# Two banks for transposed probabilities in the layers, and block 1's banded heads woven into their projections

## The reference, cut to what matters

```python
sq = partial_rope(rms_norm(grp(swa_q), q_norm_w), cos, sin)      # 3 groups x 4 heads
sk = partial_rope(rms_norm(grp(swa_k), k_norm_w), cos, sin)
...
merged = jax.nn.sigmoid(g_dn) * y_dn + jax.nn.sigmoid(g_swa) * y_swa
x = x + merged @ w_out
```

## Time and profile before

| | us |
|---|---|
| median of 3 runs | 3165.8 |
| lowest and highest | 3159.13 and 3172.29 |
| the profiled execution | 3162.07 |
| span inside the profiled execution | 3160.3 |

### The profile page before, as it was taken

The page is one execution under the profiler, slowest core; times in us unless marked ns, Lnnn a source line. Parts: engine busy times, 40 slices in busy tenths (PEclk is TensorE's granted clock), DMA queues, the critical chain, the costliest instruction groups (busy, mean ns, idle before and its releaser), DMA issues.

```text
span 3160.3 us, 36642 instructions
## 1 busy us (share of the span) xinstructions
PE 2952.1 (93%) x13424; PEld 2334.4 (74%) x13424; DVE 1468.4 (46%) x2032; ACT 1088.7 (34%) x1771; POOL 237.6 (8%) x176
## 2 busy tenths in 40 slices
PE   8878898999899999998999999899999988999998
PEld 5567676678678888566768888788886666778886
DVE  5653246853354433555444443444434545354432
ACT  4412233444223222555343332323224645332321
POOL 0000000000110012000220002100021000120012
PEclk9989899999999999999999999999999999999999
DMA  3100221213322333011212232232322110222332
GB/s 118 53 14 14 70 74 34 73 40 96 111 80 93 102 101 136 17 48 34 66 55 93 93 104 100 69 100 93 105 92 100 40 41 27 74 77 96 98 102 79
DMA packets 68356, 237.97 MB, mean 75 GB/s; under 512 B 10272, under 2 KB 12448, under 8 KB 67616
## 3 DMA queue, kind: packets, MB, share of 16 engines
q1 hardware_dynamic: 66240, 227.87, 22.3%
q10 hardware_dynamic: 2016, 8.77, 0.7%
HBM read 234.51 MB, written 2.10 MB: 75 GB/s over the span
## 4 chain that ended last, share of the span: by engine, by line
PE 65%; ACT 3%; DVE 3%; issue 2%; DMA 0%; POOLq 0%; DVEq 0%; POOL 0%; SPq 0%; PEldq 0%; ACTq 0%
PE bank L372 18%; PE bank L374 18%; PE bank L373 18%; PE bank L823 2%; PE bank L847 2%; PE bank L834 2%; PE bank L630 2%; PE bank L640 1%; PE bank L1427 1%; ACT L_w_hi L360 1%; ACT L_probsT L900 1%; PE bank L1404 0%; ACT L_job_rstd L673 0%; DVE L_h_lo L467 0%; ACT L_probs L889 0%
## 5 line engine op out<-in xcount | busy, mean ns | idle before, releaser
L372 PE MATMUL bank<-L_h_hi,L_w_hi 128*128 128x512 f32 x1776 | 703.2, 396 | 36.8 <-DVE L_weight_ring_low L366 14.0
L374 PE MATMUL bank<-L_h_hi,L_weight_ring_low 128*128 128x512 f32 x1776 | 694.8, 391 | 0.0
L373 PE MATMUL bank<-L_h_lo,L_w_hi 128*128 128x512 f32 x1776 | 694.5, 391 | 0.0
L360 ACT CAST L_w_hi<-L_weight_ring 128x1024 fp32r<-128x1024 f32 (+2 forms) x292 | 325.9, 1116 | 924.4 <-PE bank L374 915.6
L366 DVE TENSOR_TENSOR L_weight_ring_low<-L_weight_ring,L_w_hi 128x1024 fp32r<-128x1024 f32 (+2 forms) x292 | 393.8, 1349 | 380.1 <-ACT L_w_hi L360 379.7
L372 PEld LDWEIGHTS bank<-L_h_hi,L_w_hi 128*128 128x128 f32 x1776 | 335.4, 189 | 116.0 <-DVE L_weight_ring_low L366 15.7
L373 PEld LDWEIGHTS bank<-L_h_lo,L_w_hi 128*128 128x128 f32 x1776 | 335.9, 189 | 70.6 <-issue 2.4
L374 PEld LDWEIGHTS bank<-L_h_hi,L_weight_ring_low 128*128 128x128 f32 x1776 | 335.3, 189 | 70.8
L372 PE MATMUL bank<-L_act_hi,L_w_hi 128*128 128x512 f32 x704 | 273.9, 389 | 0.0
L373 PE MATMUL bank<-L_act_lo,L_w_hi 128*128 128x512 f32 x704 | 273.9, 389 | 0.0
L374 PE MATMUL bank<-L_act_hi,L_weight_ring_low 128*128 128x512 f32 x704 | 273.9, 389 | 0.0
(11 more groups left out here) (304 smaller groups left out, 3891.9 us busy)
## 6 DMA issues: line engine op xcount, KB each, us to landing
L_weight_ring<-ffn_in SPq DMA_DIRECT2D x176, 512.0 KB, 3.6
L_weight_ring<-ffn_out SPq DMA_DIRECT2D x64, 704.0 KB, 4.1
B_weight_ring<-w_sqk SPq DMA_DIRECT2D x24, 512.0 KB, 3.6
B_weight_ring<-w_dn SPq DMA_DIRECT2D x16, 512.0 KB, 3.7
B_weight_ring<-w_gate SPq DMA_DIRECT2D x16, 512.0 KB, 3.6
L_weight_ring<-w_sna_qk SPq DMA_DIRECT2D x16, 512.0 KB, 3.7
L_weight_ring<-w_mix_out SPq DMA_DIRECT2D x16, 512.0 KB, 3.6
B_weight_ring<-w_sv SPq DMA_DIRECT2D x12, 512.0 KB, 3.6
```

The source lines that it names most:

```text
L360: e.copy(hv.high(at)[:, 0:width], sh.ring[:, at % RING, 0:width]).then_inc(hv.w_hi_done, 1)
L372: e.matmul(out, a_hi, b_hi, start=start, stop=False)
L373: e.matmul(out, a_hi, b_lo, start=False, stop=False)
L374: return e.matmul(out, a_lo, b_hi, start=False, stop=stop)
```

## The change

**In the layers.** Turned probabilities go through banks 3 and 1 in turn (`at_.pt_done` starts with a credit of 2). Jobs from the sixth on all use bank 0 (`job["bank"] = 0`), and so a projection waits until DVE has read the one before it. From step 6 to 24 (`sums_first`, the new argument `early`) each engine finishes job j-1 before it begins job j. The first unit's transposes wait until the last job that used bank 1 has been read (`turn_needs`).

**In block 1.** The loop over two pairs of heads is gone. Four heads of six jobs and four units stand in one list, `sw_turns`: seven jobs and a unit; three times job, job, unit, job, job, unit, job, unit, job, unit; four units. A head's first scores wait for that head's six jobs. At steps 12, 18 and 24 the finish stands in front (`sw_first`). Jobs use banks 0 and 1 and one sum bank, 2; turned probabilities use bank 3 alone, outputs bank 4. Within a unit step the segments of `scores(u+1)` alternate with the groups of transposes of `turn(u)` (`zip_longest`); ACT and DVE run one unit ahead, not two.

**Output projection of block 1.** It writes banks 0 and 1 instead of 4 and 5. Its first tile starts when seven merged tiles are there and waits for the eighth before its last three matmuls.

```diff
-def jobs_pe_steps(e, seen, sh, jb, at, jobs, hv=None, mixed=False):
+def jobs_pe_steps(e, seen, sh, jb, at, jobs, hv=None, mixed=False, early=(), sum_banks=None):
...
+        for turn in (("finish", "begin") if j in early else ("begin", "finish")):
+            if turn == "begin" and j < len(jobs):
...
+                bank = banks[job.get("bank", j % 2)]
+                e.wait_ge(jb.gained, seen.free(jb.gained) + ("bank" in job))
...
     for u in range(n):
+        turned, scored = turn(u), scores(u + ahead) if u + ahead < n else ()
         if ahead == 2:
-            turn(u)
-        if u + ahead < n:
-            scores(u + ahead)
-        if ahead == 1:
-            turn(u)
+            for _ in itertools.chain(turned, scored):
+                pass
+        else:
+            for _ in itertools.zip_longest(scored, turned):
+                pass
...
-        at_ = Attn(sc, T, [4, 5], [3], [6, 7], big, 8 * TT)
+        at_ = Attn(sc, T, [4, 5], [3, 1], [6, 7], big, 8 * TT)
...
+            for job in mix_jobs[5:]:
+                job["bank"] = 0
...
+            mix_units[0]["turn_needs"] = [(jb.gained, jobs_before + 4)]
+            mem_units[0]["turn_needs"] = [(jb.gained, jobs_before + len(mix_jobs) + 4)]
...
+        sums_first = range(6, 2 * MLA_HEADS + 8 + 1)
...
-        at_ = Attn(sc, 1280, [5, 6, 7], [0, 1], [2, 3], big)
+        at_ = Attn(sc, 1280, [5, 6, 7], [3], [4], big)
...
+                                     needs=[(jb.done, 2 + 8 + 4 + 6 * (h + 1))] if t == 0 else []))
...
+        sw_turns = ["job"] * 7 + ["unit"]
+        sw_turns += ["job", "job", "unit", "job", "job", "unit", "job", "unit", "job", "unit"] * (NH - 1) + ["unit"] * TT
+        sw_first = range(2 * len(sw_jobs) // NH, len(sw_jobs) + 1, len(sw_jobs) // NH)
...
-                e.wait_ge(merged_done, seen.ready(merged_done, KT))
+                all_merged = seen.ready(merged_done, KT)
                 for n in range(KT):
                     e.wait_ge(sh.x_done, seen.free(sh.x_done))
                     halves_here(e, seen, sh, hv, at + n)
                     for k in range(KT):
-                        mm = halves_mm(e, banks[4 + n % 2][:, :], hv, at + n, k, merged_hi[:, k, :],
+                        if n == 0 and k in (0, KT - 1):
+                            e.wait_ge(merged_done, all_merged - (k == 0))
+                        mm = halves_mm(e, banks[n % 2][:, :], hv, at + n, k, merged_hi[:, k, :],
```

More of the change, by code:

```diff
@@ L18 @@
+import itertools
 from contextlib import ExitStack, contextmanager
@@ new lines, in jobs_act_steps @@
+        for turn in (("finish", "begin") if j in early else ("begin", "finish")):
+            if turn == "begin" and j < len(jobs):
+                job = jobs[j]
+                r0, rn = job["rows"]
+                w = job["width"]
+                e.wait_ge(sh.strip_done, seen.ready(sh.strip_done, len(job["parts"])))
+                e.wait_ge(jb.summed, seen.free(jb.summed))
+                src = sh.banks[job.get("bank", j % 2)][r0:r0 + rn, 0:w]
+                if "by" in job:
+                    e.wait_ge(jb.gained, job["number"])
+                    src = jb.g[r0:r0 + rn, j % 2, 0:w]
+                e.activation(jb.sq[r0:r0 + rn, j % 2, 0:w], src, ACT.Square).then_inc(jb.squared, 1)
+                if hv is not None and job.get("split", True):
+                    split_strip_act(e, seen, sh, hv, at + j + 2, KT * P)
+            if turn == "finish" and j > 0:
+                job, b = jobs[j - 1], (j - 1) % 2
+                w = job["width"]
+                e.wait_ge(jb.summed, seen.ready(jb.summed))
+                e.wait_ge(jb.done, seen.free(jb.done))
+                e.activation(jb.rs[:, b, 0:w], sh.banks[sum_banks[b % len(sum_banks)]][:, 0:w], ACT.Ln, scale=job["scale"],
+                             bias=EPS).then_inc(jb.lned, 1)
+                e.wait_ge(jb.lned, seen.ready(jb.lned))
+                e.activation(jb.rs[:, b, 0:w], jb.rs[:, b, 0:w], ACT.Exp, scale=-0.5).then_inc(jb.rstd, 1)
@@ L824, in scores @@
             seg[0] += 1
-        if units[u]["segs"][0][3] is not None:
-            seen.free(at_.exped)
+            yield
     def turn(u):
         e.wait_ge(at_.exped, seen.ready(at_.exped))
+        for need in units[u].get("turn_needs", ()):
+            e.wait_ge(*need)
         for ch in chunks(units[u]):
@@ L904, in attn_act_steps @@
     n = len(units)
-    for u in range(2):
+    ahead = 2 if len(units[0]["segs"]) == 1 else 1
+    for u in range(ahead):
         exps(u)
@@ L983, in attn_dve_steps @@
     yield
-    for u in range(2, n + 2):
+    for u in range(ahead, n + ahead):
         if u < n:
@@ L2425, in _ @@
                         e.copy(val[:, t, bass.ds(it * 512, 512)], banks[4 + t][:, :]).then_inc(v_done, 1)
-                j_, a_ = jl(0), al()
-                with seen.loop(e, 2, ready=merged(j_[2], a_[2]), free=merged(j_[3], a_[3])) as it:
-                    jobs_act(e, seen, sh, jb, sw_jobs, hv, V_FIRST + 12)
-                    attn_act(e, seen, sh, at_, units(it))
+                take_turns(sw_turns, job=jobs_act_steps(e, seen, sh, jb, sw_jobs, hv, V_FIRST + 12, sw_first, (2,)),
+                           unit=attn_act_steps(e, seen, sh, at_, sw_units))
                 for f in range(NH):
```

275 lines of the change are left out of this document (122 added, 153 removed).

## The result

| | us |
|---|---|
| before, median of 4 runs | 3165.4 (3159.13 to 3172.29) |
| after, median of 4 runs | 3129.5 (3127.07 to 3138.72) |
| ratio, 95% interval | 0.9903, 0.9891 to 0.9916 |
| the profiled execution after, its span | 3127.07, 3125.2 |
| after once more (experiment 5), median of 5, and before beside it, median of 9 | 3135.8, before 3161.7 |

The change makes the kernel about 0.9% faster; the second pair says 26 us, the first ratio 31. One of the ten executions of experiment 6 took 9455 us, for a reason that no run shows, and is left out there; all others agree with their like within 0.5%. The page of after: PE does the same 13424 matmuls, and the span is 35.1 us shorter.

What follows compares the result with a forecast made beforehand. PE was taken to bound the kernel, busy 93% of the span, with gains only where it waits. From 3162.1, 25 for the layers and 6.7 for the output projection came off, 0 for the weave: 3130 us, range 3106 to 3153.

Steps and rivals of the forecast that it cites:

- two of three terms: The sum's terms: 25 us off in the two layers, 6.7 off at the output projection, 0 for the weave.
- Part 1, long jobs: Layers, after long jobs: three copy waits go, five windowed ones keep 3.4 of 8.9 us; gain 9.3 us per layer.
- The early finish: Layers: Ln and Exp move ahead of ACT's square, taking 1.16 us off ACT's path to the copy.
- 3.5 against 3.1: Layers, full unit: PE wants the copy 3.5 us after a job's end; ACT's copy ends at 3.1.
- first rival: Layers: the copy is missed again, at the values; only 1.16 us go at eight places, 18.6 in all, 3137; chance 0.17.
- Part 2, units after the jobs: Layers, units behind the jobs: the second bank saves 3.2 of 7.0 us of waits per layer, bounds 0 and 7.0.
- Part 3, short jobs: Layers, short jobs: almost no PE wait there, so moving the sum gains zero, bounds -2 and +2 us.
- Part 4, output projection: Block 1: the gap shrinks to 0.6 us, saving 4.8, and absent half-clock matmuls return 1.9; gain 6.7, bounds 4.8 and 7.3.
- Part 5, the weave: Block 1: idle time 29.1 us against 28.0 before, so the weave is worth nothing, within -13 and +12.
- I expect two falls again: Block 1's weave: the clock falls twice as before, now at gaps of 5.8 and 6.8 us.
- The rule: Layers: the skill's remark that PSUM double-buffering gave no further gain with PE busy; by it the time would be 3137.

Runs made afterwards that it cites:

- experiment 5: The changed kernel with block 1's attention as before (no weave): 3129.9 us, run beside the unaltered changed kernel at 3135.8.
- experiment 6: Only block 1's output projection changed, against the kernel before: 3154.6 us against 3160.3, ratio 0.9985.
- experiment 2: Kernel before with the layers' edits but begin before finish everywhere, so the second bank without the early finish: 3133.4 us, ratio 0.9920 to before.
- experiment 3: Kernel before with the layers' edits but transposed probabilities through bank 3 alone, so the early finish without the second bank: 3160.0 us, ratio 0.9994.
- after_again: The changed kernel, unaltered, run and profiled once more: 3135.8 us against 3161.7 for before, ratio 0.9915.
- experiment 1: Kernel before with all of the layers' edits, block 1 untouched: 3136.7 us against 3161.7, ratio 0.9927.
- experiment 10: The changed kernel with two banks for block 1's turned probabilities and two instead of three for its scores: 3175.8 us, ratio 1.0056 to before.
- experiment 7: The changed kernel with the finish in front also at head 0 (step 6 of block 1): 3126.2 us against 3160.3 of before, ratio 0.9891.
- experiment 9: The changed kernel with the finish in front at head 0 too and head 3's last jobs each a unit earlier: 3132.5 us, ratio 0.9908 to before.

## Why the prediction was right, and where it wasn't

The forecast was 3130 us; the measured median is 3129.5, and 3135.8 in the second set of runs. The direction and two of three terms hold; the third was hidden by the spread. That the first median meets the forecast to 0.5 us is luck: its distance from before is 35.9 us in this set and 25.9 in the second, and the forecast takes off 32.

**Part 1, long jobs: 9.3 us per layer.** Right in mechanism. The three waits of 1.25 went; at the five windowed places 0.22, 0.33, 0.66, 2.42 and 0.66 remain, 4.3 for 3.4. The 2.42 was not foreseen: the forecast counted ACT's steps and left out that DVE's new order can make ACT's square late (experiment 2). The period is 10.66 (10.9 forecast). That a projection waits for bank 0 did not occur.

**The early finish** stands in the forecast as one of the two edits that make the gain, with 1.16 us off ACT's path. This is a step that failed inside a right sum. PE's sum moves away together with Ln and Exp, so PE comes 0.86 us earlier as well. The forecast has both shifts in its 3.5 against 3.1, but does not draw from them that only 0.3 us is left of the edit; without it the two would be 4.3 against 4.28. Three of the places of experiment 2 show that 0.3, and by the ratios the edit brings nothing that can be measured (experiments 2 and 3). With it falls the first rival's price of 18.6 us, which counted the 1.16 alone.

**Part 2, units after the jobs: 3.2 of 7.0.** 5.1 us remain in the first layer behind the last job's, so 1.9 were saved. The reason was right (the exponential comes right after the copy, 14.2 for 6.7), its size not. Parts 1 and 2 are thus 8.4 + 1.9 = 10.3 us of idle per layer, for 12.5 forecast. The second execution of the changed kernel shows just this (10.4 and 10.9). In the first another 1.6 per layer came from the wait for the residual, which fell from 5.5 to 2.4. That gain is not steady: over the ten executions with the second bank this wait is 2.4 to 5.5 us, and 5.5 in four besides `after_again`. What no term of the sum had is the cross-attention. It takes 58.3 us in either layer of before and 56.4 or 56.5 in after; over all executions it is 57.3 to 58.5 with one bank and 56.3 to 57.5 with two, so it gave 1 to 2 us per layer. That 25 us were forecast for the two layers and 25 measured (experiment 1) is in part luck.

**Part 3, short jobs: nothing.** Right; no wait stands between 1294 and 1411 us of after.

**Part 4, output projection: 6.7.** The gap fell to 0.6 and its half-clock matmuls are gone; the stage gives 6.7 in the trace and the time 5.7 (2 to 8) in the runs. The size is right, its make-up less so. Most of what the clock returned here it took later: from 855.3 us on PE is busy 1.6 us more up to the layers, and over the whole stage its busy time is only 0.3 less (590.32 to 590.02). In its place the waits for `L_h_lo` fell from 13.3 to 11.6, which was in no term. In experiment 6 it is the other way round: 1.4 us less of busy time, and 12.7 of these waits.

**Part 5, the weave: 0 (-13 to +12).** Measured +6, inside the bounds. The waits came as listed: 5.61, 0.66, 0.65 and 6.13 at the keys (5.8, 1.4, 1.4, 6.8 forecast), some 6.6 for the single bank in woven units (4.8), 6.2 in the tail (7.6), 1.0 at the store (1.3): 26.9 for 29.1. The step that failed is "I expect two falls again". In after the clock falls a third and a fourth time in the tail, at 654 and at 662, behind gaps of 2.08 and 2.15 us among small matmuls. The third:

```profile
653.61 0.66 PE L845 MATMUL bank<-shared_consts,B_arena 128*128 128x128 f32 x4 [2.08 <-ACT B_arena L903]
654.11 1.10 PE L833 MATMUL bank<-B_arena 128*128 128x512 f32 x2
...
655.91 1.92 PE L833 MATMUL bank<-B_arena 128*128 128x512 f32 x2
```

An equal pair of scores takes 1.10 and then 1.92 us. From 662 to 668 the granted clock is 0.50 again. `after_again` shows four falls as well, before and the kernel without the weave two. Over the stretch PE was busy for 3.9 to 5.6 us more than before, which the sum had at nothing.

**The rule.** The waits of transposes for copies, 39.8 us, fell with a second bank, and experiment 2 puts 25 us (by the ratio) to 28 (by the medians) on that edit. The Trainium skill's remark in "TensorE: Matmul & The Clock Gate", section "HAM oscillation — how this bites in real kernels", that PSUM double-buffering gave no further gain, is told of another matmul kernel; it is not what this one shows. The Trainium skill's "Perfetto Trace Analysis", section "Matmuls", says that independent groups should rotate through banks so that the emptying of one lies beside the next; experiment 2 agrees with it for the transposes, and experiment 10 for the scores, which lost a bank.

**The parts and the whole.** Layers -25.0, output projection -5.7 and weave +6.0 make -24.7 in medians; the changed kernel has -25.9 in the second pair and -35.9 in the first, where before ran at 3165.4 for the 3160 to 3162 of the others. So the parts add, and the first pair flattered the whole. The forecast's 32 us lies above both 26 and the 31 of the ratio. Why the changed kernel itself ran at 3129.5 once and at 3135.8 once no run shows; in the two profiled executions PE's busy time makes 4.8 of the 8.7 us between the spans.

**A better version.** Without the weave the kernel is 6 us below the changed one (3129.9 for 3135.8 on one chip, 0.9898 of before). With the weave and experiment 7's order it stands at 0.9891. The two were not run on one chip, so which is better stays open. Only the kernel without the weave is shown to be below the changed one; experiment 7's interval (0.9874 to 0.9907) overlaps with the changed kernel's.

## What to carry to other kernels

Before counting what leaves the releasing engine's path, count what leaves the waiting engine's path with it: a step that moves both wins only the difference. A second bank pays where the engine that empties the first has a long piece of other work to do first (here 2.6 to 3.7 us on ACT). A bank taken away from scores cost all that stood before the mask on DVE (up to 4.8 us), not the mask. And a rebuilt order is to be judged by idle time and by busy time: here waits fell and the stretch grew longer.

## What the runs showed of the hardware

One gap can be cheaper than its parts. In experiment 9 the longest wait of block 1 was cut up, idle time fell by 1.2 us, and 998 matmuls took 217.75 us where 997 had taken 211.25, at a mean granted clock of 0.94 for 0.97 (one execution each). In the tail of after the clock stood at its upper level while PE was only half busy, and fell right behind:

```profile
650.00:654.00 4.00, 1.92 (x14) 1.39 (x12) 2.11 (x3) 1.44 (x3) 0.00 (x0) 1.00 0.01 2
654.00:656.00 2.00, 2.00 (x10) 1.30 (x9) 0.69 (x1) 0.59 (x1) 0.00 (x0) 0.73 0.00 0
656.00:658.00 2.00, 2.00 (x5) 0.97 (x5) 0.14 (x1) 0.59 (x1) 0.00 (x0) 0.50 0.00 0
```

So the fall shows in matmuls that themselves wait for nothing.

The same work takes a different time from one execution to the next, and where no edit is at work the difference is busy time of PE. The first 430 us, up to the first sum of block 1, are alike in all kernels of this case. Their shortest and longest execution, those of experiment 10 and of before:

```profile
0.00:427.40 427.40, 361.22 (x1792) 280.56 (x1793) 192.92 (x280) 125.42 (x186) 0.20 (x4) 0.94 0.16 56
0.00:435.20 435.20, 370.57 (x1792) 285.89 (x1793) 192.94 (x280) 125.64 (x186) 0.21 (x4) 0.92 0.17 55
```

PE is busy for 9.4 us more at a granted clock of 0.92 for 0.94, and idle for 1.5 us less. The second mix took 272.5 to 275.5 us in the ten executions with the second bank. A stretch that differs by a few us between two profiled executions is therefore to be compared over several before it is put down to an edit.
